# Expert choice moved into the output projection, a shorter slot chain, and placement in steps of 128 tokens

## The reference

```python
g_idx = jnp.argmax(g_probs, axis=-1)
...
top_p, top_i = lax.top_k(f_probs, TOP_K_FINE)
top_p = top_p / jnp.sum(top_p, axis=-1, keepdims=True)
weights = (g_p * top_p).reshape(-1)
expert_ids = (g_idx[:, None] * EXPERTS_PER_GROUP + top_i).reshape(-1).astype(jnp.int32)
```

## Time and profile before

| | us |
|---|---|
| median of 3 runs | 4586.31 |
| lowest, highest | 4585.81, 4589.57 |
| profiled execution | 4583.22 |
| its span, first to last instruction | 4581.3 |
| `mix` in the span | about 2454 to 2987 |
| `route` in the span | about 2987 to 3094 |
| `experts` in the span | about 3094 to the end |

### The profile page before, as it was taken

One profiled execution on the slowest core, in us unless ns is written; L12 is line 12 of the kernel. 1 busy time (PEld: TensorE's weight loads), 2 busy tenths in 40 slices (PEclk: granted clock), 3 DMA queues, 4 the chain that ended last, 5 costly groups with the idle time before them and its releaser, 6 DMA issues. The chain is left out here.

```text
span 4581.3 us, 85648 instructions
## 1 busy us (share of the span) xinstructions
PE 4253.7 (93%) x28623; PEld 3184.9 (70%) x28625; DVE 2899.1 (63%) x3384; ACT 2542.4 (55%) x3946; POOL 605.5 (13%) x770
## 2 busy tenths in 40 slices
PE   7999979997998998999996999929999999999998
PEld 5888867775555555555554888827888788888886
DVE  3222246778998998999994333385666555555665
ACT  3222225556887887888884232214666555555665
POOL 0000002222000000000000000022233332222322
PEclk9999989998999999999998999969999999999999
DMA  4222231113011001001003333235656655555664
GB/s 137 100 108 101 78 122 55 55 55 118 24 35 57 29 29 57 29 29 50 6 9 124 129 141 134 101 119 184 245 209 226 219 196 202 201 189 182 242 246 142
DMA packets 279574, 540.01 MB, mean 118 GB/s; under 512 B 38320, under 2 KB 103856, under 8 KB 279344
## 3 DMA queue, kind: packets, MB, share of 16 engines
q1 hardware_dynamic: 228512, 410.49, 25.4%
q0 software_dynamic: 46224, 118.03, 7.5%
q10 hardware_dynamic: 4608, 8.39, 0.5%
HBM read 410.97 MB, written 176.16 MB: 128 GB/s over the span
## 5 line engine op out<-in xcount | busy, mean ns | idle before, releaser
L1036 DVE TENSOR_TENSOR_SCAN att_R<-att_stay,att_R 128x512 f32<-128x512 f32 x896 | 1058.9, 1260 | 27.4 <-ACT att_stay L976 25.3
L986 ACT ACTIVATE att_RT<-att_rt 128x512 f32<-128x512 f32 (+3 forms) x1152 | 585.9, 562 | 233.3 <-PE att_rt L927 203.1
L927 PEld LDWEIGHTS att_rt<-ident,att_R 64*128 64x128 f32 x8448 | 319.4, 139 | 373.2 <-issue 369.5
L976 ACT ACTIVATE att_stay<-att_z 128x1024 f32<-128x1024 f32 (+2 forms) x576 | 554.5, 963 | 24.4 <-PE att_z L914 22.9
L940 PE MATMUL att_out<-att_RT,att_dv 128*64 128x512 f32 (+3 forms) x2304 | 520.6, 573 | 0.1
L927 PE MATMUL att_rt<-ident,att_R 64*128 64x64 f32 x8448 | 383.7, 227 | 99.7 <-ACT att_RT L986 55.8
L1348 DVE TENSOR_TENSOR ew_lo<-ew_raw,ew_hi 128x1024 fp32r<-128x1024 f32 x372 | 430.2, 1218 | 13.6 <-ACT ew_hi L1341 13.6
L1341 ACT ACTIVATE ew_hi<-ew_raw 128x1024 fp32r<-128x1024 f32 x384 | 373.7, 1047 | 97.3 <-PE ex_down L1771 97.3
L243 PE MATMUL qkv_out<-qkv_u_hi,qkv_w_hi 128*128 128x512 f32 x768 | 312.2, 406 | 8.0 <-DVE qkv_u_lo L234 8.0
L243 PE MATMUL qkv_out<-qkv_u_hi,qkv_w_lo 128*128 128x512 f32 x768 | 302.8, 394 | 0.0
L243 PE MATMUL qkv_out<-qkv_u_lo,qkv_w_hi 128*128 128x512 f32 x768 | 301.6, 393 | 0.0
(11 more groups left out here) (261 smaller groups left out, 8418.8 us busy)
## 6 DMA issues: line engine op xcount, KB each, us to landing
ew_raw<-in_w_e_gate SPq DMA_DIRECT2D x32, 2048.0 KB, 9.3
ew_raw<-in_w_e_up SPq DMA_DIRECT2D x32, 2048.0 KB, 9.5
ew_raw<-in_w_e_down SPq DMA_DIRECT2D x32, 2048.0 KB, 9.1
qkv_x<-in_x SPq DMA_DIRECT2D x32, 512.0 KB, 4.8
lru_x<-in_x SPq DMA_DIRECT2D x32, 512.0 KB, 4.7
mix_raw<-s_mix_t SPq DMA_DIRECT2D x32, 512.0 KB, 4.1
mix_x<-in_x SPq DMA_DIRECT2D x32, 512.0 KB, 4.8
s_h<-mix_h SPq DMA_DIRECT2D x32, 512.0 KB, 3.5
```

Source lines behind the costliest of these rows:

```text
L927: last = nc.tensor.transpose(rt[half][:, h, qt, :], R[lanes, n % 3, h, qt, s * P:(s + 1) * P], k.ident[lanes, lanes])
L976: done = nc.scalar.activation(pair(stay[:, step % 4, :]), pair(z[step % 2][:]), ACT.Sigmoid, scale=-scale)
L986: nc.scalar.activation(RT[:, :, s, first:, half, :], rt[half][:, :, first:, :], ACT.Copy).then_inc(rt_copied[half], 1)
L1036: nc.vector.tensor_tensor_scan(R[:, n % 3, h, s, 0:width][:, ::-1], src[:, ::-1], src[:, ::-1], initial, ALU.mult, ALU.bypass).then_inc(sc ...
```

## The change

What it does, part by part:

- The choice of experts leaves `route`. A new function `select` in `mix` makes it for four token tiles at a time, 21 chained VectorE instructions over at most 128 x 128 numbers, placed behind the first tile's `u2` of the next loop turn; the last one stands alone at the end of `mix`. It leaves `k.first`, `k.both`, `k.dist`, `k.g_dist`. The iota is made there too (on GpSimd), and ScalarE's square of `h` goes into `u2` in place of a scratch tile.
- In `route` TensorE can start at once: totals first, in the order expert by tile, so that the prefix sum reads PSUM directly; then the in-tile counts with a matrix (`k.rest`) that already takes off the tile's own total. The copy of the totals and the subtraction go. Row and lane are formed once for both choices.
- In placement VectorE no longer multiplies by the weight. ScalarE does, with one 128 x 98 instruction for each 128 tokens (64 in all), and TensorE waits for each.
- GpSimd has no weight work in `route`. ScalarE splits matrix 0 of expert 0 ahead of placement and matrices 1 and 2 behind it; the lower parts (12 pieces) are computed by VectorE at the start of `experts`, behind the index of `h`. SyncE loads expert 1's weights in `experts`, each matrix when the lower part of expert 0's is done.

```diff
@@ mix
-            junk = sb("mix_junk", [P, D])
+            SELECT_STEPS = 21
...
+            def select(dve, G):
+                def link(instruction):
+                    count[0] += 1
+                    instruction.then_inc(select_step, 1)
+                    dve.wait_ge(select_step, G * SELECT_STEPS + count[0] + 1)
...
+                dve.wait_ge(logits_ready, G * TT + TT + 1)
+                link(V.tensor_reduce(s_max[:], logit[:, :, 0:NGRP], AX.X, ALU.max))
...
+                link(V.tensor_tensor(grouped(s_fine[:]), grouped(logit[:, :, NGRP:]),
+                                     s_pen[:].unsqueeze(3).to_broadcast([P, TT, NGRP, EPG]), ALU.add))
+                for c in range(TOPK):
...
+                    link(V.tensor_reduce(s_top[c][:], s_fine[:], AX.X, ALU.max))
+                    link(V.tensor_tensor(s_eq[:], s_fine[:], spread(s_top[c][:], NE), ALU.is_equal))
+                    link(V.scalar_tensor_tensor(s_eq[:], s_eq[:], -2.0 * NE, along(NE), ALU.mult, ALU.add))
+                    link(V.tensor_reduce(first, s_eq[:], AX.X, ALU.min))
+                    link(V.tensor_tensor(found[:], s_eq[:], spread(first, NE), ALU.is_equal))
...
-                    nc.scalar.activation(junk[:], h[:, t, :], ACT.Square, accum_out=sum2[:]).then_inc(squared, 1)
+                    nc.scalar.activation(u2[:, t, :], h[:, t, :], ACT.Square, accum_out=sum2[:]).then_inc(squared, 1)
...
+                    if t == 0 and not first:
+                        select(dve, G - 1)
...
+                dve.wait_ge(select_step, (NG - 1) * SELECT_STEPS + 1)
+                select(dve, NG - 1)
@@ route
-            for m in range(MATRICES):
-                weights.low(pool, m, 0)
...
-            for e in range(2):
-                weights.load(sp, e)
+            weights.load(sp, 0)
...
-            for m in range(MATRICES):
+            weights.high(act, 0, 0)
+            for turn in range(TOPK * NT // BT):
+                c, t = divmod(turn * BT, NT)
+                act.wait_ge(coded, turn + 1)
+                for i in range(BT):
+                    row = row_facts[turn % 2][:, i, 1, :]
+                    nc.scalar.activation(row, row, ACT.Copy, scale=weight[:, c, t + i:t + i + 1]).then_inc(hot_ready, 1)
+            for m in range(1, MATRICES):
                 weights.high(act, m, 0)
...
-            pe.wait_ge(both_ready, 1)
+            by_expert = k.both[:].rearrange("p (t e) -> p e t", e=NE)
             for i in range(2):
-                nc.tensor.matmul(prefix[i][:], k.before[:], both[:, i * GT:(i + 1) * GT], start=True, stop=True)
+                last = nc.tensor.matmul(total[:, i * GT:(i + 1) * GT], k.ones_bf[:], by_expert[:, i * NE // 2:(i + 1) * NE // 2, :],
+                                        start=True, stop=True)
+            last.then_inc(counted, 1)
...
-                pe.wait_ge(hot_ready, turn + 1)
                 for t in range(BT):
+                    pe.wait_ge(hot_ready, turn * BT + t + 1)
...
+            for c in range(TOPK):
+                link(V.scalar_tensor_tensor(hot[c], along(NE), -2.0 * NE, spread(k.first[:, c, :], NE), ALU.add, ALU.is_equal))
...
             dve.wait_ge(counted, 1)
-            for i in range(2):
-                half = NT // 2
-                link(V.tensor_copy(totals[:, :, i * half:(i + 1) * half], total[i][:].rearrange("p (t e) -> p e t", e=NE)))
-            flat = lambda ap: ap[:].rearrange("p e t -> p (e t)")
-            link(V.tensor_tensor_scan(flat(upto), flat(seg), flat(totals), 0.0, ALU.mult, ALU.add))
-            link(V.tensor_tensor(base[:], upto[:], totals[:], ALU.subtract))
+            link(V.tensor_tensor_scan(sums[:, 1, :], seg[:].rearrange("p e t -> p (e t)"), total[:], 0.0, ALU.mult, ALU.add))
...
+            link(V.tensor_copy(slot_i[:], slot_f[:]))
+            link(V.tensor_scalar(lane_i[:], slot_i[:], P - 1, None, ALU.bitwise_and))
...
-                link(V.tensor_tensor(rows[:, :, 1, :], rows[:, :, 1, :], wide(weight[:, c, t:t + BT], WIDE), ALU.mult))
-                done(hot_ready)
+                done(coded)
@@ experts
+            weights.load(sp, 1)
             with sp.Fori(2, NE) as e:
                 weights.load(sp, e)
...
             dve.wait_ge(params, 16)
+            dve.wait_ge(h_index_ready, 1)
+            weights.low(dve, 0, 0)
             x_low(dve, 0)
+            for m in range(1, MATRICES):
+                weights.low(dve, m, 0)
```

## The result

The changed kernel takes 4548.9 us (median of four executions, 4547.56 to 4550.51) against 4587.41 us for the kernel before beside it: a ratio of 0.9916, 95% interval 0.9904 to 0.9928. It is faster by 38.5 us. The forecast was 4546.2, the range 4539 to 4555.

A forecast was written before the change was run, and what follows sets the result against it. VectorE's chain in `route` was taken as the bound there (TensorE in the output projection). Choice +5.9, chain -43.8, placement -7.0 and end +4.8 sum to -40.1 us: 4586.31 - 40.1 = 4546.2 us, range 4539 to 4555.

The forecast's parts named there:

- What bounds the kernel: In `route`, one VectorE chain of about 104 us bounds; whatever leaves it leaves the total, unless another engine ends the stage.
- Choice in `mix`: In `mix`, a call takes 5.9 us (bounds 4.2 and 6.7); seven are covered, the eighth, standing alone, costs +5.9.
- The cover of 11.8: In `mix`, TensorE first asks for the split tile after 11.8 us free; a call stalls it only beyond that.
- The chain: `route` up to placement: 19.1 us in place of 62.9, -43.8.
- Placement: Placement in `route`: 28.6 us in place of 35.6 for 8 turns, -7.0.
- The end: End of `route`, last turn to GpSimd's first index: ScalarE is late, 11.2 us in place of 6.4, +4.8.
- Start of `experts`: Start of `experts`: the split of gathered rows comes 0.4 us late, at 8.3, and the moved weight work costs nothing.
- The sum: Whole kernel: 5.9 - 43.8 - 7.0 + 4.8 = -40.1 us, 4546.2 us against the median; chance 0.80.
- Placement paced by small steps: Rival in placement: with 64 waits TensorE's turns stay at 4.8 us, +7.2, 4553.4 us; chance 0.08.
- slower by the links: Rival in `mix`: links waiting on loop-counter values last longer; at 1.1 us each the kernel takes 4625 us; chance 0.03.
- `experts` pays back: Rival in `experts`: the second gather is held until VectorE's splits end, about +5, 4551 us; chance 0.05.
- No cover: Rival in `mix`: each in-loop call stalls TensorE by its whole length, +1.2 in all, 4587.5 us; chance 0.04.

The follow-up runs named there:

- second run: The changed kernel, unchanged, measured a second time beside the kernel before: 4548.26 us, ratio 0.9909.
- e5: Kernel after with 24 more chained VectorE sums of 128 x 128 numbers behind each choice: 4593.63 us, ratio 1.0012.
- e10: Kernel after with 12 more chained VectorE sums of 128 x 128 numbers behind each choice: 4559.56 us, ratio 0.9938.
- e1: Kernel before with only GpSimd's weight work taken out of `route` and put where the changed kernel has it: 4563.51 us, ratio 0.9948.
- e8: Kernel after with twelve GpSimd subtractions, which read and write SBUF, added in `route`: 4564.1 us, ratio 0.9948.
- e9: Kernel after with twelve GpSimd memsets, which only write constants, added in `route`: 4561.46 us, ratio 0.9939.
- e3: Kernel after with all twelve upper pieces of ScalarE's splits ahead of placement: 4544.79 us, ratio 0.9904.
- e7: Kernel after with one wait of TensorE a turn for all eight of ScalarE's products: 4555.02 us, ratio 0.9927.
- e6: Kernel after with the choice made once in `route` for all 32 tiles, and none of it in `mix`: 4559.83 us, ratio 0.994.

## Why the prediction was right, point by point

- **What bounds the kernel.** Right: `route`'s chain on VectorE left the total one for one. Choice to end fell by 39.7 us and the median by 38.5 (39.7 in the second run), where 40.1 were forecast.
- **Choice in `mix`.** The eighth call was forecast at +5.9 and cost 8.84 - 2.85 = 6.0. The seven others cost some 0.7 us together, at most 1.4, where nothing was forecast. Six of them took 7.5 us and the seventh 6.9, not 5.9, above the upper bound of 6.7. The step that failed is the price of a link (one instruction of the chain): each of the seven calls holds one that meets GpSimd, 1.1 to 1.2 us in place of 0.17, and the six in the loop have 0.1 to 0.2 more of gap in several. The eighth call, with no GpSimd work beside it, has neither. The cover of 11.8 was read off one tile; e5 and e10 put it at 10.4 where the clock is full. The forecast held since 7.5 fits in both covers of the split tile. It doesn't fit in the 6.7 us before the second half's sum moves; that sum came later, and TensorE never waited for it.
- **The chain.** Forecast 19.1, measured 19.03. The prefix sum was 2.29 for 2.45, the small steps 0.22 from start to start as taken. That the 2.27 us steps were GpSimd's doing was argued from rows 5 alone; e1, e8 and e9 show it.
- **Placement.** Forecast 28.6, measured 29.64, within the bounds. The mis-sized term is the first turn of TensorE, 5.50 us for 4.79, so that VectorE's third turn starts 9.29 us into placement and not 8.5. Its mean granted clock was 0.52 where it had been 0.60, and over the twelve profiles of this study the first turn takes 4.53 to 5.59; no run asks why the full clock comes sooner or later. The later turns have a period of 3.39 for 3.35; ScalarE's product is 2.25 / 8 = 0.28 for 0.30.
- **The end.** Forecast 11.2, measured 10.52: the pieces took 7.66 as forecast, the barrier 0.76 where 1.0 was taken, the last products 2.1 from VectorE's end (2.5). That ScalarE would be late next was right. What the prediction didn't ask is whether the pieces had to stand there; e3 shows that they didn't have to.
- **Start of `experts`.** Right in each row: 8.2 for 8.3 to the split of the rows, 20.1 for 20.4 to the second transposes, `experts` 1486.84 against 1487.37.
- **The rivals.** *Placement paced by small steps* and *slower by the links* are ruled out for this kernel by its own rows; e7 shows that coarser waits would be the slow ones, and e5 that a choice twice as long takes the whole gain (4593.63 us, ratio 1.0012). *`experts` pays back*: the second gather wasn't held, but it was issued 0.26 us before the eight splits began, so this row doesn't show one that is asked for in their midst. Later rows do: a GpSimd copy that starts inside a split (3103.22 to 3104.44) takes 1.01 us, where its median in `experts` is 0.18, and GpSimd's gathers of `u2` that start inside one are issued in 1.12 us, the others in 0.99 (medians). A hold exists, then, but it costs a gather 0.13 us and not the rest of eight splits. *No cover*: e6 shows the cover, for `mix` is no more than 1.4 us shorter without any choice in it.
- **The sum.** Against the median before of these runs, 4587.41, the sum gives 4547.3, 1.6 us below the 4548.9 measured; the kernel after a second time had 4548.26 against 4587.92. The terms' own errors nearly cancel, which is luck between placement and the end (+0.1 choice, -0.1 chain, +1.0 placement, -0.7 end, -0.5 `experts`). The profiled span fell by only 35.6 because "start" was 4.65 later, in stages ahead of `mix`; with it left out it is 40.2, as forecast. Why "start" differs between executions stays open.

## What to carry to other kernels

When a chain of small VectorE instructions runs beside GpSimd work, look for steps that last as long as one GpSimd piece: moving GpSimd's work out of that stretch was worth 23 us here, more than all shortening of the chain (putting such work back cost 15 in the shorter chain). Work that is hidden under TensorE is free only up to the moment at which TensorE next asks for something queued behind it, and that moment comes sooner where the clock is full: measure the cover on several tiles and take the shortest. When work is moved off the bounding engine, ask at once what the engine that takes it had to do there, and whether that can go ahead of it and not behind.

## What was not expected of the hardware

- GpSimd instructions that only write SBUF stall VectorE as much as those that read it (16.0 and 15.3 us in the same chain), but only its casts and steps of one input with constants: up to 2.25 us for a cast of 32 numbers that takes 0.18 without them, while two-input steps keep their 0.19.
- TensorE's waits can cost more than their length. After waits of 2.28 and 3.02 us in placement 16 matmuls took 4.6 us and not 2.92, and the loop of `mix` lost 32.2 us where its waits are 24.9, at a mean granted clock of 0.90 for 0.94.
